# Index pick of a product-key retrieval in fp16 pairs, with all 128 projection dots of the gathered tile in the projection stage

## What is computed

```python
q = (hf @ w_q).reshape(T, PEER_HEADS, 2, PEER_HALF)             # 8 heads, 2 halves
sc = einsum('thpc,hpnc->thpn', q, sub_keys)                     # 128 keys in each half
s_top, i_top = top_k(sc, 16)
cand = s_top[:, :, 0, :, None] + s_top[:, :, 1, None, :]        # 16 x 16 pairs of keys
ids_cand = i_top[:, :, 0, :, None] * 128 + i_top[:, :, 1, None, :]
s_fin, pos = top_k(cand, 16)
ids = take_along_axis(ids_cand, pos)                            # the index pick
gates = softmax(s_fin)
a = gelu(einsum('cd,ckd->ck', xc, expert_u[ids]))               # 128 experts for each token
y = einsum('ck,ckd->cd', gates * a, expert_v[ids])
```

## Time and profile before

| | us |
|---|---|
| median of 3 runs | 1884.44 |
| lowest, highest | 1862.87, 1893.11 |
| the profiled execution | 1857.03 |
| its span, first to last instruction | 1855.0 |
| busy in it: PE, DVE, POOL, ACT | 1727.8, 1260.0, 1147.0, 745.9 |
| mean granted TensorE clock | 0.98 of full speed |

### The profile page before, as it was taken

One profiled execution on the slowest core, in us unless ns is written; L12 is line 12 of the kernel. 1 busy time (PEld: TensorE's weight loads), 2 busy tenths in 40 slices (PEclk: granted clock), 3 DMA queues, 4 the chain that ended last, 5 costly groups with the idle time before them and its releaser, 6 DMA issues.

```text
span 1855.0 us, 27166 instructions
## 1 busy us (share of the span) xinstructions
PE 1727.8 (93%) x9077; PEld 1476.4 (80%) x9077; DVE 1260.0 (68%) x2106; ACT 745.9 (40%) x1105; POOL 1147.0 (62%) x701
## 2 busy tenths in 40 slices
PE   6988999999999999999499999998999999999997
PEld 5766778888788999999399999986677677677775
DVE  6678521221221599999999999437878788787887
ACT  5477632322332333333166666432333233333333
POOL 6522224444333477887477777677778788788783
PEclk9999999999999999999699999999999999999999
DMA  6211122222212458788489999988979999899993
GB/s 238 91 46 46 35 69 93 100 95 97 91 68 89 130 178 273 247 271 278 142 273 358 336 353 335 354 312 317 342 288 338 346 351 350 313 351 355 345 337 128
DMA packets 145537, 424.77 MB, mean 229 GB/s; under 512 B 15312, under 2 KB 64464, under 8 KB 143312
## 3 DMA queue, kind: packets, MB, share of 16 engines
q1 hardware_dynamic: 108336, 289.46, 45.2%
q0 software_dynamic: 36864, 134.23, 19.0%
q10 hardware_dynamic: 288, 0.54, 0.1%
HBM read 371.74 MB, written 52.43 MB: 229 GB/s over the span
## 4 chain that ended last, share of the span: by engine, by line
PE 47%; DVE 29%; DMA 9%; ACT 5%; issue 4%; POOL 3%; DVEq 1%; SPq 1%; ACTq 0%
PE both L504 14%; PE bank L515 9%; DVE wf L1492 7%; DMA a_in<-a_rows 7%; PE bank L504 7%; PE bank L519 4%; DVE both L1508 4%; DVE rows L1377 3%; PE bank L814 3%; PE bank L797 2%; POOL w_lo L458 2%; ACT wT_hi L1093 2%; DVE cand L1360 2%; PE bank L714 2%; DVE cand L1417 2%
## 5 line engine op out<-in xcount | busy, mean ns | idle before, releaser
L458 POOL TENSOR_TENSOR w_lo<-raw,w_hi 128x1024 fp32r<-128x1024 f32 (+1 forms) x430 | 865.3, 2021 | 641.9 <-ACT w_hi L862 640.7
L862 ACT ACTIVATE w_hi<-raw 128x1024 fp32r<-128x1024 f32 x346 | 365.8, 1058 | 545.7 <-PE bank L519 238.0
L515 PE MATMUL bank<-hT_hi,w_hi 128*128 128x384 f32 x1024 | 348.6, 340 | 6.6 <-ACT abuf L1060 6.6
L515 PE MATMUL bank<-hT_lo,w_hi 128*128 128x384 f32 x1024 | 343.3, 335 | 0.0
L479 POOL DMA_INDIRECT rows<-stream,idx x256 | 278.1, 1086 | 49.5 <-issue 24.1
L814 PE MATMUL bank<-w_hi,wT_hi 128*128 128x512 f32 x768 | 212.4, 412 | 45.6 <-ACT wT_hi L1093 44.2
L1492 DVE TENSOR_TENSOR wf<-a_in,g_in 128x384 f32<-128x384 f32 x128 | 200.9, 1570 | 67.7 <-DMA a_in<-a_rows 65.9
L814 PEld LDWEIGHTS bank<-w_hi,wT_hi 128*128 128x128 f32 x768 | 136.2, 189 | 117.9 <-ACT wT_hi L1093 92.6
L1093 ACT ACTIVATE wT_hi<-wf 128x384 fp32r<-128x384 f32 x128 | 66.9, 523 | 372.6 <-DVE wf L1492 372.4
L515 PEld LDWEIGHTS bank<-hT_hi,w_hi 128*128 128x128 f32 x1024 | 193.2, 189 | 9.0 <-issue 8.8
L814 PE MATMUL bank<-w_hi,wT_lo 128*128 128x512 f32 x768 | 198.3, 393 | 0.2 <-DVE wT_lo L1496 0.2
(11 more groups left out here) (249 smaller groups left out, 2212.1 us busy)
## 6 DMA issues: line engine op xcount, KB each, us to landing
raw<-stream SPq DMA_DIRECT2D x346, 512.0 KB, 3.8
a_rows<-abuf SPq DMA_DIRECT2D x128, 192.0 KB, 5.3
g_rows<-gstage SPq DMA_DIRECT2D x32, 768.0 KB, 7.9
g_in<-g_rows SPq DMA_DIRECT2D x16, 1536.0 KB, 9.4
a_in<-a_rows SPq DMA_DIRECT2D x128, 192.0 KB, 5.5
rows<-stream,idx POOLq DMA_INDIRECT x256, 6.6
x_sb<-x SPq DMA_DIRECT2D x4, 512.0 KB, 8.5
out<-x_sb SPq DMA_DIRECT2D x4, 512.0 KB, 2.6
```

Source lines behind the costliest of these rows:

```text
L458: last = pool.tensor_tensor(w_lo[:, k % 2, cols], raw[:, k % RAW, cols], w_hi[:, k % 2, cols].bitcast(f32), ALU.subtract)
L515: pe.matmul(dst, w_hi[:, slot, k * P:(k + 1) * P], hT[low][:, k, DENSE], start=(k == 0 and low == 0), stop=False)
L862: act.activation(w_hi[:, base % 2, :], raw[:, slot, :], ACT.Copy).then_inc(hi_ready, 1)
```

## The change

- The pick works on both halves at once and in fp16. Positions of both halves are shifted or masked, cast once to f16 (`fsel2`), and compared with a 16 x 16 table `grid16`, in the order [head, a, k] in place of [head, k, a] (k is the place in the result, a the candidate). The key indices lie as pairs of equal f16 values (`top2`), so that the product reads in pairs. The sum over a then walks `chosen` with a step of 16 elements. A drain comes after each pair of operations.
- 18 projection dots in place of 12 in each of retrievals 1 to 3 (54), 48 with the gates, and all other 26 in the tail; none in the value stage. Value dots start at chunk 4, at 16 in 15 chunks.
- The first eight gathers stand together behind chunk 12; the next ones start behind chunk 14, at 11 in 10 chunks; those of the tail go at 9 in 5 chunks.
- 68 plain chunks and a tail of 12. SP's step 9 stays step 9.
- GT is overwritten with its own remainder, in place of a second tile R1; `first_id` takes the place of fself for the ids.

```diff
@@ constants and schedules
-I_PLAIN, I_GATES = 64, 48
+I_PLAIN, I_GATES = 68, 48
...
-TOP_DOTS, TAIL_DOTS = 12, 12
+TOP_DOTS = 18
 GATE_DOTS0 = (TT - 1) * TOP_DOTS
-LATE_DOTS0 = GATE_DOTS0 + I_GATES + TAIL_DOTS
-GELU_I = 28
-GATHER_C = 14
+TAIL_DOTS0 = GATE_DOTS0 + I_GATES
+GELU_I = 4
+GATHER_C = 12
 
 
 def late_dots(i):
 
-    if i < GELU_I - 2:
-        return min(HK, LATE_DOTS0 + (i + 1) * 4 // 3)
-    return min(2 * HK, HK + max(0, i - GELU_I + 1) * 4 // 3)
+    return min(2 * HK, HK + max(0, i - GELU_I + 1) * 16 // 15)
 
 
 def gather_after(g):
 
+    if g < SLOTS:
+        return GATHER_C
     if g < GATE_DOTS0:
-        return GATHER_C + 2 + g * 13 // 10
-    if g < LATE_DOTS0:
+        return GATHER_C + 2 + (g - SLOTS) * 10 // 11
+    if g < TAIL_DOTS0 + SLOTS:
         return I_PLAIN + g - GATE_DOTS0 - SLOTS + 2
+    if g < HK:
+        return I_PLAIN + I_GATES + 2 + (g - TAIL_DOTS0 - SLOTS) * 5 // 9
     return NI - 4 + next(i for i in range(NI) if late_dots(i) > g)
@@ tiles, and the tables that POOL's iota writes
-        iota_k = keep("iota_k", [TOPK])
+        grid16 = keep("grid16", [TOPK, TOPK], f16)
...
+        chosen = Place(r.at)("chosen", [2, PEER_H, TOPK, TOPK], f16)
...
-        topf = r("topf", [PEER_H, 2, TOPK])
+        top2 = r("top2", [2, PEER_H * TOPK, 2], f16)
...
+            pool.iota(grid16[:, :, :], pattern=[[1, TOPK], [0, TOPK]], base=0, channel_multiplier=0,
@@ retrieve
-                dve.tensor_copy(topf[:, :, :, :], topi[:, :, :, :])
+                for q in range(2):
+                    dve.tensor_copy(top2[:, q, :, :].rearrange("p (h a) e -> p h a e", a=TOPK),
+                                    topi[:, :, q, :].unsqueeze(3).broadcast_to([P, PEER_H, TOPK, 2]))
...
+                dve.tensor_scalar(fsel[:, 0, :], fpos[:, :], 4, None, ALU.logical_shift_right)
+                dve.tensor_scalar(fsel[:, 1, :], fpos[:, :], TOPK - 1, None, ALU.bitwise_and)
+                dve.drain()
+                dve.tensor_copy(fsel2[:, :, :], fsel[:, :, :])
+                dve.drain()
+                for q in range(2):
+                    dve.tensor_tensor(chosen[:, q, :, :, :],
+                                      fsel2[:, q, :].rearrange("p (h k) -> p h k", k=TOPK).unsqueeze(2).broadcast_to(grid),
+                                      grid16[:, :, :].unsqueeze(1).broadcast_to(grid), ALU.is_equal)
+                dve.drain()
+                by_two = [P, PEER_H * TOPK, TOPK // 2, 2]
+                for q in range(2):
+                    picked = chosen[:, q, :, :, :].rearrange("p h a (k e) -> p (h a) k e", e=2)
+                    dve.tensor_tensor(picked, picked, top2[:, q, :, :].unsqueeze(2).broadcast_to(by_two), ALU.mult)
+                dve.drain()
                 for q, dst in ((0, IF), (1, JF)):
...
-                    dve.tensor_copy(fself[:, :], fsel[:, :])
-                    dve.drain()
-                    dve.tensor_tensor(pick, fself[:, :].unsqueeze(2).broadcast_to(flat),
-                                      iota_k[:, :].unsqueeze(1).broadcast_to(flat), ALU.is_equal)
-                    dve.drain()
-                    dve.tensor_tensor(pick4, pick4, topf[:, :, q, :].unsqueeze(2).broadcast_to(grid), ALU.mult)
-                    dve.drain()
-                    dve.tensor_reduce(dst[:, t, :], pick, AX.X, ALU.add)
-                    dve.drain()
+                    dve.tensor_reduce(dst[:, t, :].rearrange("p (h k) -> p h k", k=TOPK),
+                                      chosen[:, q, :, :, :].rearrange("p h a k -> p h k a"), AX.X, ALU.add)
+                dve.drain()
@@ dots after the gates, and in the value stage
-            for k in range(TAIL_DOTS):
-                expert_dot(0, GATE_DOTS0 + I_GATES + k)
+            for k in range(TAIL_DOTS0, HK):
+                expert_dot(0, k)
...
                 while dots < late_dots(i):
-                    if dots < HK:
-                        expert_dot(0, dots)
-                    else:
-                        value_dot(dots - HK)
+                    value_dot(dots - HK)
                     dots += 1
```

More of the change, by code:

```diff
@@ L199, in build @@
         topi = r("topi", [PEER_H, 2, TOPK], u32)
-        topf = r("topf", [PEER_H, 2, TOPK])
+        top2 = r("top2", [2, PEER_H * TOPK, 2], f16)
         fin = r("fin", [PEER_H, TOPK])
         fpos = r("fpos", [HK], u32)
-        fsel = r("fsel", [HK], u32)
-        fself = r("fself", [HK])
+        fsel = r("fsel", [2, HK], u32)
+        fsel2 = r("fsel2", [2, HK], f16)
+        first_id = r("first_id", [HK])
         scur2 = cand2
@@ L208, in build @@
         GT = o("GT", [TD])
-        R1 = o("R1", [TD])
         gsm = o("gsm", [TT * PEER_H])
@@ L448, in _ @@
                       allow_small_or_imprecise_dtypes=True)
-            pool.iota(iota_k[:, :], pattern=[[1, TOPK]], base=0, channel_multiplier=0,
+            pool.iota(grid16[:, :, :], pattern=[[1, TOPK], [0, TOPK]], base=0, channel_multiplier=0,
                       allow_small_or_imprecise_dtypes=True)
@@ L1381, in _ @@
             grid = [P, PEER_H, TOPK, TOPK]
-            flat = [P, HK, TOPK]
-            pick = cand[:, :, :].rearrange("p h (k a) -> p (h k) a", a=TOPK)
             pick4 = cand[:, :, :].rearrange(all2, a=TOPK)
@@ L1425, in _ @@
             for q, first_row in enumerate((CHUNKS * P, S_EV * P)):
-                dve.tensor_scalar(fself[:, :], IF[:, 0, :], float(P), float(first_row), ALU.mult, ALU.add)
+                dve.tensor_scalar(first_id[:, :], IF[:, 0, :], float(P), float(first_row), ALU.mult, ALU.add)
                 dve.drain()
-                dve.tensor_tensor(idx[:, q, :], fself[:, :], JF[:, 0, :], ALU.add)
+                dve.tensor_tensor(idx[:, q, :], first_id[:, :], JF[:, 0, :], ALU.add)
                 dve.drain()
@@ L1448, in _ @@
             dve.wait_ge(spread_read, 1)
-            step(dve.tensor_tensor(R1[:, :], GT[:, :], G2[:, 0, :, 0], ALU.subtract))
-            step(dve.tensor_copy(G2[:, 1, :, :], pairs(R1[:, :])))
+            step(dve.tensor_tensor(GT[:, :], GT[:, :], G2[:, 0, :, 0], ALU.subtract))
+            step(dve.tensor_copy(G2[:, 1, :, :], pairs(GT[:, :])))
             keys = [P, TOK_I, NKEYS // 2, 2]
@@ L1510, in value_dot @@
                 last.then_inc(dotted, 1)
-            dots = LATE_DOTS0
+            dots = HK
             for i in range(NI):
```

5 lines of the change are left out of this document (removed).

## The result

| | us |
|---|---|
| changed kernel: median of 4 runs, lowest, highest | 1904.74, 1899.69, 1904.91 |
| the kernel before beside it: median of 4 runs | 1873.65 |
| ratio, 95% interval | 1.019 (1.011 to 1.027) |
| profiled execution after: time, span | 1904.76, 1902.8 |
| busy in it: PE, DVE, POOL, ACT | 1747.6, 1312.8, 1136.8, 748.2 |

The changed kernel is 1.9% slower; the forecast was 1889 us, within a range of 1862 to 1918.

The account below looks back on a forecast made before the run. Bounds: DVE's retrievals in the plain part, PE, DVE and transfers together in the gates, a lock step in the value stage. 8.8 + 9.5 - 13.3 = +5.0 us on 1857.0 gave 1862.0, 1889 on the median's scale; range 1862 to 1918.

Parts of the forecast that it names:

- the 27 us that I added: Whole run: the profiled execution stood 27 us below the runs' median, 1884.4, so 1862.0 became 1889 us.
- The step that failed: Projection with gates: each of 48 chunks keeps one dot and one gather, so the change there costs nothing.
- Plain part: Projection before the gates: POOL waits for ids and dots in front of PE, +8.8 us (+2.5 to +15.1).
- p: Retrieval: one new index pick with POOL silent, 12.8 us (10.7 to 14.9) against 15.6.
- 4 of contention: Retrieval: POOL's work lengthens a pick by 4 us, against 7.8 before, as two-input work falls from 9.2 to 4.9 us.
- the factor of three: Plain part: dot 36, the first of retrieval 3, starts at 815.5 + 3p, so three picks lie ahead of it.
- my middle: Pick: each strided f16 reduction takes 3.35 us, midway between 2.29 and 4.4.
- Tail and turn: Last gate product to first value product: tail net +2, late reload and dot 127 at the turn 7.5, together +9.5 us.
- rival 3: Tail: transfers bind, 22.3 MB at 349 GB/s take 64 us; +18 for tail and turn, 1898 us, chance 0.15.
- Value stage: 128 gathers and dots, not 160; steps of 4.50 and 4.90 us plus 14.2 of other waits: 588.9 us, -13.3.
- Rival 1: Plain part: POOL's waits fit its lead and PE's idle time before the transposes goes, -46, 1838 us; chance 0.14.
- Rival 2: Pick gets no shorter: f16 at one element a cycle, reductions 4.4, p 19.4, contention 8; +33, 1917 us; chance 0.13.

Follow-up runs that it names:

- e3: Changed kernel with four plain chunks, not two, between transposes and first gate products, and ACT's exponential four chunks earlier: 1869.62 us, ratio 0.999.
- e12: Changed kernel with I_SPREAD = 0, so no plain chunk is left between transposes and gates: 1880.50 us, ratio 1.010.
- e8: Changed kernel with the lead of e3, contiguous pick of e6, early reload of e5, early gathers spread, gated-part gathers one chunk later: 1860.98 us, ratio 0.998.
- e6: e3 with the pick in the order [head, k, a], so that reductions read adjacent elements: 1863.16 us, ratio 0.998.
- e1: Kernel before with the new fp16 pick alone, old schedule kept: 1857.77 us, ratio 0.995.
- e5: Changed kernel with SP's reload of g and a at step 5 of the tail, not step 9: 1904.76 us in one run.
- e7: Kernel before with I_SPREAD = 4 alone, four plain chunks left behind the wait for the retrieval, not two: 1870.32 us, ratio 1.004.
- e9: Kernel before with I_SPREAD = 0 alone, no plain chunk left behind the wait for the retrieval: 1864.05 us, ratio 1.003.
- e11: Kernel before with the contiguous fp16 pick of e6 and I_SPREAD = 4, nothing else: 1849.01 us, ratio 0.994.

## Why the prediction held, point by point

The time came out 15.7 us above the forecast and inside the range, and within 2% of the kernel before. The sum behind it doesn't deserve that: it missed a term of 26 us. On the profiled execution's own scale the sum gave 1862.0 us and 1904.76 were measured, 42.8 more. What hid most of this is the 27 us that I added because that execution stood so far below the median of three runs. The changed kernel has no such distance (1904.76 in the profile, 1904.74 the median), so it is luck that the time fell near the forecast. "Within 2%" hangs on the same: beside the two short runs of the kernel before, 1859.07 and 1862.87, the changed kernel is 2.4% slower.

*The step that failed* is "The change leaves each of its 48 chunks with one dot and one gather, so I cost it at nothing." The number of operations did stay; the lead with which DVE enters didn't, and nothing in my text asked for it., with three resources full at once, could have been the warning. The 48 chunks took 5.76 us each in place of 5.13. e3 and e12 show the cost from either side: 269.9 us of gates become 241.3.

*Plain part.* The mechanism (POOL waits for ids and dots in front of PE) came as told: a wait of 19.2 us for w_lo of chunk 13, 4.9 for chunk 15, none for FV. e8 shows it by removing it: 7.0 us of such waits, where e6, with the same pick and the same lead, has 28.6. The size was off by 9.7 us. Dot 36 started at 867.20; with the front's 5.5 us I had 859.4. Of the 7.8 between, 1.5 were there at dot 0, and the second and third pick took 20.0 and 20.7 us from FV to the next dot where I had 17.1 (p, 4 of contention, 0.3 for FV). The pick with POOL silent was 13.4 us in place of 12.8 (the first: 15.4 less 2.0 by which one cast was stretched; the last of e1, beside which POOL only issued gathers, took 13.4 too), as its two reductions took 3.8 to 4.2 us and not 3.35; that is 0.6 of each. The larger part is contention, 6.3 and 7.0 us where I took 4: I had scaled it with the two-input work, but FV (1.72 in place of 0.29 us) and once the cast (3.19 in place of 0.29) were stretched as well. e6 shows the factor of three. The last 1.9 us lie between dot 36 and the transposes. The rule of the Trainium skill that I had set beside the sum (Vector Engine (DVE) Microarchitecture Reference, "Measured stream behaviour on trn2", 1.73 ns an element for a read that hops) gave 3.7 us, nearer than my middle; the trace has 1.9 to 2.0 ns. The Trainium skill's figure is for 32-bit words with a hop of 4 KiB, not for f16 with a step of 16 elements.

*Tail and turn.* +15.5, in my bounds (4 to 18), but not for the reason given. I let PE's time set the tail and the reload the turn. e5 moved the reload and won nothing. From the last gate product to the first value product went 69.4 to 72.6 us in all fourteen profiles, with 16 chunks and 12 dots or with 12 and 26: the four chunks taken out of the tail gave nothing back. That is nearer to rival 3 and its 18 us than to my 9.5, though not by its numbers: the changed kernel moved some 25 MB there, at 368 GB/s on the average (258 in the first 16 us, then 403 to 413), where it had 22.3 MB at 349. That the transfers are the cause is argued, as said at e5.

*Value stage.* The steps of wT_hi took 582.8 us against 602.2, so -19.4 where I had -13.3. The median step was 4.53 us, against 4.58 before; my 4.63 was a mean of three. That makes 6 us, and the other 13 come from what single steps took beyond the median, 21 us in all before and 8 after, where I had kept my 14.2. By the marks of the table it is -17.9, since the first wT_hi and the first value product stood closer together.

*Rivals.* Rival 1's idle PE went, but the time went to POOL's waits, as forecast. Rival 2's condition held in part: two f16 products of 2048 elements took 2.36 us, not the 4.7 of its 9.4 for four, but its reductions of 4.4 and its contention of 8 were nearer to the 4.15 and 6.3 to 7.0 measured than my 3.35 and 4.

*What stays open.* The two groups of the kernel before are 32.7 us apart by their means, near the 28.6 that the slow rhythm costs, and neither e7, e9 nor any combination had a run in an upper group in ten. But one of e12's six runs took 1897.13 us, 17 above the mean of the other five (1879.7), though its profile (1885.23) has the fast rhythm. The 32.7 us fit a kernel that in some executions enters with too little slack, perhaps where its two chunks behind the idle time run at full clock (13.5 us to the first gate product and not 16.0). But no profile of it was taken in the upper group, and e12's long run has none either, so this is a guess.

## What to carry to other kernels

Where two or three engines are full at once, the slack at the entry of the loop is a term of the sum: take from the trace how long before its reader each operand is done, in the first periods and in the steady state. The same instructions ran at two paces here. A gather or other wait in an in-order stream belongs behind the moment its input is there, not ahead of it; and a stage whose transfers are full may not get shorter by having its compute moved out: four chunks less gave nothing back here. Keep the reduced axis innermost: of the 291.4 us from the projection's first product to the transposes the fp16 pick took 10.5 with the strided reduction (e1) and 21.6 with adjacent elements (e11).

## What the runs showed of the hardware

- One loop of PE, ACT, POOL and DVE had two stable periods, 5.13 and 5.76 us, with identical instructions; slacks of 0.8 and of 3.5 us at the second product went with different ones, and a longer wait of PE (e12) gave a shorter run.
- A reduction of 2048 f16 elements with a step of 16 elements took 3.79 to 3.81 us in the six cases of all profiles in which PE stood still (as both in e1's last pick) and 4.0 to 4.3 us beside PE's work, whether POOL was at work or not; which part of what goes with PE's work slows it is not shown. With adjacent elements it took 2.27 to 2.29 throughout, about the same as in f32: f16 made the products faster (2.36 us for two, against 2.29 for one), not the reduction.
- PE's idle time ahead of the gates lowered the granted clock (0.54 of full speed from 882 to 910 us in the kernel before, 0.85 to 926), and the two chunks behind it took 16.0 us, where the changed kernel took 13.5 at a clock of 1.00; DVE was 6.7 us ahead at the first gate product in place of 3.3.
